# A three-block transformer kernel in fp32: another order in the differential attention, lighter VectorE work in the two mixers, and six rotations by DMA row swaps

## The reference, cut to what matters

```python
def _rope(x, pos):                      # half = d // 2
    x1, x2 = xf[..., :half], xf[..., half:]
    return jnp.concatenate([x1 * cos - x2 * sin, x2 * cos + x1 * sin], axis=-1)

def _diff_attention(q, k, v, lam, sub_g, lam_init):
    ...
        p = _masked_softmax(s, t[:, None] >= pos[None, :])
        a = p[:, :, 0] - lam * p[:, :, 1]
        return jnp.einsum('bhqk,bhkd->bhqd', a, v)
...
def _compress(x, pe, w1, w2):           # 32-token blocks, stride 16
    ...
    return jax.nn.silu(flat @ w1) @ w2
```

## Time and profile before

| | us |
|---|---|
| median of 3 runs | 2774.49 (2774.3 to 2775.41) |
| the profiled execution | 2776.58 |
| its span, first to last instruction | 2775.2 |
| TensorE busy in the span | 2712.5 (98%) |
| VectorE busy | 1667.2 (60%) |
| ScalarE busy | 1024.0 (37%) |
| mean granted TensorE clock | 0.992 |

### The profile page before, as it was taken

One profiled execution on the slowest core, in us unless ns is written; L12 is line 12 of the kernel. 1 busy time (PEld: TensorE's weight loads), 2 busy tenths in 40 slices (PEclk: granted clock), 3 DMA queues, 4 the chain that ended last, 5 costly groups with the idle time before them and its releaser, 6 DMA issues.

```text
span 2775.2 us, 35300 instructions
## 1 busy us (share of the span) xinstructions
PE 2712.5 (98%) x14529; PEld 2218.1 (80%) x14529; DVE 1667.2 (60%) x3377; ACT 1024.0 (37%) x1745; POOL 15.8 (1%) x47
## 2 busy tenths in 40 slices
PE   8999999999999999889999999999999989999999
PEld 5788888899888897666888889888888666888888
DVE  6776555357766456778776736753355778633334
ACT  4642332444222244455422224322234455422223
POOL 1000000000000000000000000000000000000000
PEclk9999999999999999999999999999999999999999
DMA  7246333224555232200555524533232310233231
GB/s 249 91 167 184 107 92 98 76 92 167 187 188 186 84 118 80 84 32 31 182 182 183 196 84 139 202 122 106 91 104 89 94 43 31 68 96 102 92 102 65
DMA packets 340360, 325.24 MB, mean 117 GB/s; under 512 B 9442, under 2 KB 332774, under 8 KB 340200
## 3 DMA queue, kind: packets, MB, share of 16 engines
q1 hardware_dynamic: 340116, 322.97, 36.1%
q10 hardware_dynamic: 84, 0.02, 0.0%
HBM read 320.87 MB, written 2.10 MB: 116 GB/s over the span
## 4 chain that ended last, share of the span: by engine, by line
PE 88%; DVE 7%; ACT 3%; SPq 1%; issue 0%; DMA 0%; DVEq 0%
PE bank L535 25%; PE bank L537 24%; PE bank L536 24%; PE bank L577 3%; PE bank L563 2%; PE bank L564 2%; PE bank L565 2%; PE bank L2319 1%; PE bank L2348 1%; DVE w_lo L503 1%; ACT E L2122 1%; PE bank L1373 1%; PE bank L1363 1%; DVE tmp L713 1%; DVE h_lo L702 1%; DVE E L2445 0%
## 5 line engine op out<-in xcount | busy, mean ns | idle before, releaser
L535 PE MATMUL bank<-h_lo,w_hi 128*128 128x512 f32 (+1 forms) x2448 | 929.4, 380 | 7.7 <-DVE h_lo L702 7.3
L537 PE MATMUL bank<-h_hi,w_lo 128*128 128x512 f32 (+1 forms) x2448 | 902.1, 369 | 0.0
L536 PE MATMUL bank<-h_hi,w_hi 128*128 128x512 f32 (+1 forms) x2448 | 901.1, 368 | 0.0
L503 DVE TENSOR_TENSOR w_lo<-raw,w_hi 128x1024 fp32r<-128x1024 f32 (+1 forms) x422 | 490.8, 1199 | 300.9 <-ACT w_hi L497 300.7
L497 ACT ACTIVATE w_hi<-raw 128x1024 fp32r<-128x1024 f32 (+1 forms) x422 | 421.5, 1035 | 341.9 <-PE bank L537 326.6
L535 PEld LDWEIGHTS bank<-h_lo,w_hi 128*128 128x128 f32 x2448 | 463.0, 189 | 94.7 <-issue 10.3
L536 PEld LDWEIGHTS bank<-h_hi,w_hi 128*128 128x128 f32 x2448 | 463.0, 189 | 79.3 <-issue 7.2
L537 PEld LDWEIGHTS bank<-h_hi,w_lo 128*128 128x128 f32 x2448 | 462.1, 189 | 77.5
L535 PE MATMUL bank<-a_lo,w_hi 128*128 128x512 f32 (+1 forms) x1056 | 390.8, 370 | 0.0
L537 PE MATMUL bank<-a_hi,w_lo 128*128 128x512 f32 (+1 forms) x1056 | 384.6, 364 | 0.0
L536 PE MATMUL bank<-a_hi,w_hi 128*128 128x512 f32 (+1 forms) x1056 | 384.4, 364 | 0.0
(11 more groups left out here) (311 smaller groups left out, 2600.1 us busy)
## 6 DMA issues: line engine op xcount, KB each, us to landing
swf<-in_w_ada SPq DMA_DIRECT2D x60, 1024.0 KB, 7.5
raw<-in_ffn_w_gate SPq DMA_DIRECT2D x44, 1024.0 KB, 5.4
raw<-in_ffn_w_up SPq DMA_DIRECT2D x44, 1024.0 KB, 5.4
raw<-in_w_in SPq DMA_DIRECT2D x40, 1024.0 KB, 5.1
raw<-in_ffn_w_down SPq DMA_DIRECT2D x32, 1024.0 KB, 5.0
raw<-in_w_in SPq DMA_DIRECT2D x34, 512.0 KB, 5.0
raw<-in_ffn_w_down SPq DMA_DIRECT2D x16, 768.0 KB, 4.2
mw<-in_w_mod SPq DMA_DIRECT2D x8, 1024.0 KB, 11.3
```

Of the source, the lines that this page charges most:

```text
L503: nc.vector.tensor_tensor(o, r, half(w_his[place_of[i]], i, h)[0].bitcast(F32), ALU.subtract).then_inc(*w_lo.up((i, h)))
L535: nc.tensor.matmul(o, w1, al, start=start, stop=False)
L536: nc.tensor.matmul(o, w1, ah, start=False, stop=False)
L537: return nc.tensor.matmul(o, w2, ah, start=False, stop=stop)
```

## The change

- **Six rotations without PE** (p = 4 to 9 of each mixer). The signed permutation becomes a plain swap of the 32-row halves: SP issues four DMAs of 32 x 512 from `tmp` into a new tile `swap` (`sp_rope`), the sign moves into the sine table, and DVE multiplies `swap` by it. PE's matmul and its bank are gone for these. The order of SP: after the load that follows nq0, nq1 and kk the swaps of two rotations each.
- **Key rotations in one addition.** `ks` and `kw` are written by one 128 x 512 addition; the second copy of each group on the other half of the partitions is made by two DMAs for each tile (`sp_cross`), for which the score matmuls wait (`cross_in`), and the matmul picks its columns by group and half.
- **Order inside a differential step.** Reciprocals and lambda product of item s - 1 stand between the two score reads of step s, and ACT's scaling of the first map between the two exponents of step s.
- **Silu of the compression.** exp(-h), then ln(1 + that), then exp of its negative, all on ACT; DVE only multiplies. For m = 1 ACT does it one step earlier (step 0).
- **`VB` in one product** of 128 x 512: the compressed values, broadcast four times, by a 0/1 table `quad`; GpSimd no longer zeroes it.
- **The mask `c01` is dropped**; a factor `any` that is zero for queries with no compressed block goes into the gate product (still one instruction).

```diff
+    def sp_rope(l, p):
+        sp.wait_ge(act, ("rq", l, p))
+        for i in range(4):
+            nc.sync.dma_start(swaps[p % 2][i * 32:i * 32 + 32, :], pair(p)[0][(i ^ 1) * 32:(i ^ 1) * 32 + 32, :]).then_inc(
+                *swap_in[p % 2].up((l, p), 16))
...
-            kd = (ks, kw)[p - 8]
-            d = [(slice(g * 64, g * 64 + 64), kd[par * 64:par * 64 + 64, g * 512:g * 512 + 512])
-                 for g in range(2) for par in range(2)]
+            d = [(every, (ks, kw)[p - 8][:, 0:512])]
...
+        else:
+            q0 = swaps[p % 2]
+            dve.wait_ge(swap_in[p % 2], (l, p))
+            nc.vector.tensor_tensor(q0[:, :], q0[:, :], sin, ALU.mult).then_inc(*dve.up(("rs", l, p)))
...
+        def factors(n):
+            ...
+            dve.wait_ge(act, ("de", l, n, 1))
+            nc.vector.reciprocal(st[:, 2:4], st[:, 2:4]).then_inc(*dve.up(("dr", l, n)))
+            dve.wait_ge(dve, PREV)
+            nc.vector.tensor_tensor(st[:, 3:4], st[:, 3:4], lv[:, 6:7], ALU.mult).then_inc(*dve.up(("dl", l, n)))
...
+                    if m:
+                        factors(s - 1)
...
+                    if m:
+                        first_map(s - 1)
...
-        nc.scalar.activation(gmb[0:64, 0:256], hsum[0:64, :], use(ACT.Exp), scale=-1.0).then_inc(*act.up(("hs", l, m)))
+        nc.scalar.activation(z, hsum[0:64, :], use(ACT.Exp), scale=-1.0).then_inc(*act.up(("h3", l, m)))
+        act.wait_ge(act, PREV)
+        nc.scalar.activation(z, z, use(ACT.Ln), bias=ones[0:64, 0:1]).then_inc(*act.up(("h4", l, m)))
+        act.wait_ge(act, PREV)
+        nc.scalar.activation(z, z, use(ACT.Exp), scale=-1.0).then_inc(*act.up(("hs", l, m)))
...
-        nc.vector.tensor_scalar(z, z, 1.0, None, ALU.add).then_inc(*dve.up(("h3", l, m)))
-        nc.vector.reciprocal(z, z).then_inc(*dve.up(("h4", l, m)))
...
+        nc.vector.tensor_tensor(VB[:, :].rearrange("p (g q d) -> p g q d", g=2, q=4),
+                                ps.of(("hv", l))[:, 0:128].rearrange("p (g d) -> p g d", g=2).unsqueeze(2).to_broadcast(at4),
+                                cst["quad"].unsqueeze(1).unsqueeze(3).to_broadcast(at4), ALU.mult).then_inc(
+                                    *dve.up(("vb", l), lets=("hv", l)))
...
+            pe.wait_ge(cross_in[br], l)
...
+                k0 = (g ^ par) * 512
...
-                nc.vector.tensor_tensor(lC, lC, g4[:, b, :, 0], ALU.mult).then_inc(*dve.up(("cg", l, b)))
-                nc.vector.tensor_tensor(e3, e3, c01, ALU.mult).then_inc(*dve.up(("cz", l, b)))
+                nc.vector.scalar_tensor_tensor(lC, lC, cst["any"][:, b:b + 1], g4[:, b, :, 0], ALU.mult, ALU.mult).then_inc(
+                    *dve.up(("cg", l, b)))
...
-            if s == 1:
+            if s == 0:
                 act_hidden_silu(l, 1)
...
+    def sp_cross(l):
+        for n, kd in enumerate((ks, kw)):
+            sp.wait_ge(dve, ("rd", l, 8 + n))
+            for par in range(2):
+                r, o = slice(par * 64, par * 64 + 64), slice(64 - par * 64, 128 - par * 64)
+                nc.sync.dma_start(kd[r, 512:1024], kd[o, 0:512]).then_inc(*cross_in[n].up(l, 16))
```

More of the change, by code:

```diff
@@ L373, in build @@
     kcz = here("kcz", 128)
-    VB = [here(f"VB{i}", 256) for i in range(2)]
+    VB = here("VB", 512)
     hid, hsum = [here(f"hid{i}", 128) for i in range(2)], here("hsum", 256)
@@ L389, in build @@
     dk = sb("dk", 1024, at=at_a + 8192)
+    swaps = [sb(f"swap{i}", 512, at=at_a + 16384 * i + 12288) for i in range(2)]
     groups = vector_rows(A)
@@ L2091, in dve_da @@
                                                        *dve.up(("dm", l, s, m), lets=("ds", l, s, m)))
+            elif s == 16:
+                factors(15)
             da_copy(dve, l, s - 3)
```

86 lines of the change are left out of this document (42 added, 44 removed).

## The result

The changed kernel takes **2742.30 us** in the median of its runs (2741.07 to 2742.89), the kernel before 2774.39 us beside it (2774.01 to 2775.41). The ratio is 0.9883, with a 95% interval of 0.9866 to 0.9900: 32.1 us faster, against 31.6 us forecast. The profiled execution took 2742.52 us with a span of 2741.2 us and a mean granted clock of 0.996 (before: 2775.2 us and 0.992), 34.1 us less than the profiled one of before.

A forecast was written before the change was run, and what follows sets the result against it. PE was taken as the bound, 98% busy, with waits mostly on late DVE and low clock behind them. Per mixer 5.2 + 4.2 + 1.7 + 4.7 = 15.8 us, 31.6 for two, gave 2743 us; range 2722 to 2760 us.

The forecast's parts named there:

- The list of eight waits: PE's waits in the first mixer: eight of 0.47 to 4.35 us, 16.5 us in all, seven ending on DVE.
- Part 1: Six rotation matmuls per mixer leave PE for DMA swaps: 6 x 0.86 = 5.2 us gained, swaps costing nothing.
- the 5.2 us are inside stretches where PE sets the pace: Claim that all six dropped rotation matmuls of a mixer lie where PE sets the pace between its waits.
- I cost the queue at nothing: Claim that swaps on SP's queue delay no weight load issued behind them: 0 us.
- Part 2: Differential attention: less DVE work and the new order shorten PE's waits by 4.2 us a mixer.
- The 2.2 us wait on ACT's copy as it is: Differential attention: PE's wait for ACT's copy of a transposed item stays, hanging on step-15 reads behind rotation 9.
- Part 3: Differential attention: the low-clock stretch behind the 4.35 us wait goes, 1.7 us a mixer.
- Part 4: NSA: silu, mask and `VB` savings cut PE's waits by 3.9 us, low clock by 0.8: 4.7 us a mixer.
- larger gain: Rival: DVE entirely off the path, more waits and low clock go, 2725 to 2734, say 2730 us; chance 0.20.
- DVE stays the pacemaker: Rival: reciprocals ahead of the second score read hold it up in differential attention; smaller gain, 2751 us; chance 0.25.
- DVE off the path: Rival: step-15 copy wait and half the NSA waits go too, clock stays up; say 2730 us; chance 0.20.
- Slower: Rival: swaps landing after more than about 10 us stall DVE and PE at rotations, 2797 us; chance 0.04.

The follow-up runs named there:

- e11: Changed kernel with later NSA weight splits, vv and w1 loads in plain order, earlier ACT copies and compressed-score exponent, earlier DVE copies in two NSA steps: 2728.59 us.
- e9: Changed kernel with each rotation's swap cut into 8 DMAs of 16 rows instead of 4 of 32: 2750.61 us.
- e10: Changed kernel with each rotation's swap cut into 16 DMAs of 8 rows: 2790.47 us, ratio to the kernel before 1.0052.
- e2: Changed kernel with the six rotations of each mixer back on PE, without swap DMAs: 2748.82 us.
- e5: Kernel before with only the six rotations by DMA swaps (old order, silu, mask, value copies and four key additions): 2772.11 us.
- e12: e11 with the six rotations of each mixer back on PE: 2735.31 us.
- e8: Changed kernel with DVE's weight splits of the gu and first o1 units moved to later NSA steps: 2737.27 us.
- e4: Changed kernel with the eight copies for `VB` and the 0/1 mask product back: 2745.64 us.

## Why the prediction was right, point by point

**The total: right, and by two errors of opposite sign.** 15.8 us for a mixer were forecast and 18.8 and 17.8 measured, 36.6 instead of 31.6 us; 2.5 us came back outside the mixers in the profiled executions. I had forecast nothing there. The profiled execution of before is also 2.2 us above its median and that of after 0.2 us, so the medians differ by 32.1 us and not by 34.1. That the forecast of 31.6 us comes so close is luck. Every experiment's first mixer also starts 0.6 to 2.9 us later than that of before, ahead of the mixer's work that the change alters; why, no run settles.

**What bounds the kernel: right, with three things overlooked.** The list of eight waits leaves out two that the timeline of before shows (0.88 us at 1179.46 and 0.68 us at 1203.39), and the list of slices one at a lowered clock:

```profile
1220.00:1224.00 4.00, 3.90 (x15) 2.74 (x16) 3.86 (x10) 1.20 (x4) 0.00 (x0) 0.58 0.00 0
```

All three are still there in the kernel after (0.87 us, 0.68 us, and the stretch behind the 2.76 us wait), so they change nothing in the sum. The waits fell where DVE was late, and in e11, with nearly all of them gone, PE's clock is 0.999 and the time is 2728.6 us.

**Part 1, the rotations: right as to the swap, over-valued as to the matmul.** No DVE wait on a swap exists, and none of PE on a crossing. Rotation 5 is indeed the tightest; its copy on ACT and its sine product on DVE, in the two timelines of the kernel after, against the earlier trace rows:

```profile
1079.85 0.60 ACT L1993 ACTIVATE tmp<-bank 128x512 f32<-128x512 f32 x1 [0.18 <-PE bank L542]
1088.42 0.69 DVE L2021 TENSOR_TENSOR swap<-swap,l2t 128x512 f32<-128x512 f32 x1
```

From 1080.45 to 1088.42 us are 8.0 us of cover (forecast "still 7"), and the swap needs 4.4 us of them (forecast 3.8): its last copy is issued at 1082.84 us, and a landing, counted from the start of the issue, is 2.0 us. One issue took 1.14 us there; where each takes 0.6 us, as at rotation 7, it is 3 x 0.6 + 2.0, some 3.9 us. The landing, 2.3 us by the earlier trace rows, was 2.0. The issue was 0.59 us and not the 0.37 us of the earlier trace rows: that row is a load from HBM that SP issued with nothing just before it. A load straight behind another took 0.57 us (1086.27 us), and the first copy of a group 0.51 and 0.61 us (1092.83 and 1073.08 us), so both the neighbour and the kind of transfer have a part. The Trainium skill ("DMA: Bandwidth & Descriptors", section "Anatomy of one DMA — SWDGE (gpsimd) path") gives about 2.0 us of fixed time per DMA, for DMAs that GpSimd issues, which the prediction did not say. Here SP issues, and the trace has 2.0 us too, from the start of the issue to the landing. The estimate of 8.6 us for four in series does not hold, since they overlap in all but their issue. The Trainium skill's advice in the same page's "Rules for kernel authors", that transfers under 64 KB pay mostly overhead, does not touch the swaps of 64 KB; for the 32 and 16 KB of e9 and e10 the trace agrees, as issue time on a shared queue.
The step that failed is "the 5.2 us are inside stretches where PE sets the pace". Put back they cost 2.9 and 1.7 us (e2; the 1.7 holds a piece of luck with the clock, see there), alone they bring 3.1 (e5), and in the kernel with the fewest waits 3.9 and 3.3 (e12). In the sum of the changed kernel the 5.2 us are there in full, but beside them stand waits (0.98 and some 0.6 us) that would not be there with the rotations on PE.
"I cost the queue at nothing" held by 0.6 us (e8, e9). I had looked at the loads behind each pair of swaps and their events, and not at when PE would want the last of them.

**Part 2, DVE in the differential attention: right.** The scaling wait went from 18.0 to 7.7 us (forecast: by about 9). The 4.35 us wait left some 0.6 us (forecast 1.2), the 0.52 and 0.47 us ones are gone. "The 2.2 us wait on ACT's copy as it is" failed: 1.11 us is left, but there is 0.98 us at a copy six steps earlier. Both hang on the copy's place behind ACT's exponents: in e11, where it stands ahead of the second one, they are 0.28 and 0.62 us (e11 has other edits too, so this is likely rather than shown). DVE's addition for a key rotation is one row now, against the earlier trace rows; `VB` likewise:

```profile
1128.99 0.69 DVE L2024 TENSOR_TENSOR ks<-swap,tmp 128x512 f32<-128x512 f32 x1
1177.63 0.69 DVE L2314 TENSOR_TENSOR VB<-bank,res 128x512 f32<-128x512 f32 x1 [0.98 <-PE bank L2305]
```

**Part 3, and the clock in part 4: the term mis-sized.** 1.7 + 0.8 = 2.5 us of a mixer were forecast. The low clock fell from 17.1 to 6.8 us, so 5.15 us. The low stretch behind the wait on ACT's copy was forecast to stay (1.7 us of work); it went when that wait fell to 1.11 us. Of the 6.8 us around 1184 us (1182.4 to 1189.2 us) one half went, 1.7 us of work where 0.8 was forecast; the other half stands behind the 2.09 us wait, from 1169.0 to 1172.4 us. This is part of the step by which the "larger gain" comes, without the rest: the NSA waits stayed. Its reason, that a stretch that goes prevents the next, is not shown by any run.

**Part 4, NSA: right in sum.** From the first NSA scores to its full part 5.0 us were gained, 4.7 forecast, and 13.8 us before that, where 11.1 were. The waits of 2.35 and 2.36 us fell to 0.2 and 2.09 (together 2.4 us, 2.3 forecast); the 3.04 us one to 2.76 (0.3 us, 0.4 forecast), the 1.20 us one is gone.

**The rivals.** "DVE stays the pacemaker" by a reciprocal that holds up the score read: no such wait shows. Its sum counts 2.6 us for the early rotations, but only two of the six stand before step 8 (1078.84 and 1083.64 us), 1.7 us, which makes it 2753 and not 2751 us. "DVE off the path" came about in e11 only, by other edits, at 2728.6 us where 2725 to 2734 had been worked out. "Slower" was made in e10.

## What to carry to other kernels

An instruction's worth is not its length but its place: 4.2 us of VectorE work in the late part of its queue was worth 4.4 to 4.6 us of a mixer, while 5.2 us of matmuls on the busiest engine was worth 2.9 to 3.9 us (1.7 us in the one mixer that was lucky with the clock), because waits for VectorE grow as TensorE's work shrinks. Work the sum with the engine that is late, add to each wait that goes the low clock behind it, and expect parts put back one at a time to add up to more (here 40 us) and parts tried alone to less (11 us) than the change (32). When a matmul is turned into DMAs, reckon the issue time on the queue with the copy's own duration and follow every load queued behind it to the engine that wants it: the transfers had 8.0 us of cover and needed 4.4, but the weight behind them was in time by 0.6 us only.

## What the runs showed of the hardware

Copies from SBUF to SBUF, from the list of DMA issues of the kernel after (count, KB each, median us to landing), and of e9:

```profile
swap<-tmp SPq DMA_DIRECT2D x48, 64.0 KB, 2.0
ks<-ks SPq DMA_DIRECT2D x4, 128.0 KB, 6.8
```
```profile
swap<-tmp SPq DMA_DIRECT2D x96, 32.0 KB, 2.0
```

64 and 32 KB land in 2.0 us alike, so the size does not matter there; 128 KB took 6.8 us for `ks` and 3.6 us for `kw`, issued just behind three loads of 2 MB in all, with the DMA engines full (DMA share 1.10 from 1132 to 1136 us); that the loads are the reason is likely, not shown. An issue of such a copy holds SP for 0.59 us (0.62 us with 8 rows each) and a load from HBM for 0.37 us when SP has nothing else before it, 0.57 us straight behind another load.

Not every wait of TensorE is followed by a low clock: in the kernel after the waits of 0.98 and 1.11 us had none, and 2.09 and 2.76 us had 3.4 us each, which is 1.7 us of work lost on top of the wait. Nor is the low clock a fixed price of a wait: the 2.76 us had none behind it in the second mixer of e2, and the same 2.36 us wait of e4 had 6.8 us in the first mixer and 3.4 us in the second. So 1.7 us of a mixer can come from the clock alone, with the waits unchanged.
